# Dilated attention: scores of the two heads of a pair issued in turn on the two halves of the array rows, items two by two every second slot

## What is computed

```python
def dilated_mixer(h, w_in, w_out):
    proj = (h @ w_in).reshape(B, S, N_GROUPS, 3, N_HEADS, HEAD_DIM)   # 3 groups, q/k/v, 16 heads of 64
    for g, (window, dil) in enumerate(((128, 1), (512, 4), (2048, 16))):
        q, k = partial_rotary(proj[:, :, g, 0], pos), partial_rotary(proj[:, :, g, 1], pos)
        o, lse = dilated_band_attention(q, k, proj[:, :, g, 2], dil, window // dil)
    wts = softmax(stack(lses)); o = einsum('gbsh,gbshd->bshd', wts, stack(outs))
    return o.reshape(B, S, ATTN_WIDTH) @ w_out
```

## Time and profile before

| | |
|---|---|
| median of three runs | 2191.45 us |
| the profiled execution | 2191.2 us, with a span of 2189.4 us |
| mean granted TensorE clock | 0.981 of full speed |
| TensorE matmul busy | 2077.3 us (95%) |
| VectorE busy | 1226.0 us (56%) |
| ScalarE busy | 1011.4 us (46%) |
| DMA | 354.16 MB, 162 GB/s |

### The profile page before, as it was taken

How to read it: one execution, slowest core, us unless ns; L and a number is a source line. 1 busy time by engine, 2 the same in 40 slices (tenths; PEclk the granted TensorE clock), 3 DMA queues, 4 the chain that set the end, 5 groups by cost and what they waited for, 6 DMA issues and landing times.

```text
span 2189.4 us, 27184 instructions
## 1 busy us (share of the span) xinstructions
PE 2077.3 (95%) x9866; PEld 1711.1 (78%) x9866; DVE 1226.0 (56%) x1352; ACT 1011.4 (46%) x1257; POOL 237.8 (11%) x351
## 2 busy tenths in 40 slices
PE   6999988989999999979999999999999999999997
PEld 5887867778887887867778877888878887888886
DVE  4555579865455555579865554444445545445544
ACT  4444663544444435754544444444435444454442
POOL 1000067000000000086000001111100000000000
PEclk9999999999999999999999999999999999999999
DMA  5554442545544554442444544333334554414552
GB/s 226 203 184 172 173 151 97 186 157 192 187 182 176 179 191 182 158 155 97 183 172 182 187 177 154 120 131 119 130 118 154 191 189 148 163 58 178 187 192 86
DMA packets 53861, 354.16 MB, mean 162 GB/s; under 512 B 7824, under 2 KB 8464, under 8 KB 11920
## 3 DMA queue, kind: packets, MB, share of 16 engines
q1 hardware_dynamic: 53776, 353.04, 43.8%
HBM read 351.97 MB, written 1.05 MB: 161 GB/s over the span
## 4 chain that ended last, share of the span: by engine, by line
PE 81%; DVE 8%; ACT 4%; issue 3%; DVEq 2%; POOL 1%; POOLq 1%; DMA 0%; ACTq 0%; SPq 0%
PE psum L1641 56%; PE psum L1697 16%; DVE wlo L959 3%; DVE arena L1134 2%; DVEq L1128 2%; ACT whi L551 2%; PE psum L1707 1%; PE psum L2038 1%; PE psum L1739 1%; PE psum L2018 1%; PE psum L1653 1%; PE psum L2025 1%; POOL arena L1509 1%; PE psum L1787 1%; PE psum L1816 0%
## 5 line engine op out<-in xcount | busy, mean ns | idle before, releaser
L959 DVE TENSOR_TENSOR wlo<-raw,whi 128x2048 fp32r<-128x2048 f32 x325 | 744.3, 2292 | 441.4 <-ACT whi L551 441.1
L1641 PE MATMUL psum<-whi,xTh 128*128 128x512 f32 (+1 forms) x1936 | 776.3, 401 | 30.7 <-DVE xTl L966 17.5
L1641 PE MATMUL psum<-whi,xTl 128*128 128x512 f32 (+1 forms) x1936 | 755.3, 390 | 0.0
L1641 PE MATMUL psum<-wlo,xTh 128*128 128x512 f32 (+1 forms) x1936 | 754.1, 389 | 0.0
L551 ACT ACTIVATE whi<-raw 128x2048 fp32r<-128x2048 f32 x325 | 621.0, 1916 | 272.6 <-PE psum L1697 151.0
L1641 PEld LDWEIGHTS psum<-whi,xTh 128*128 128x128 f32 x1936 | 368.2, 190 | 108.4 <-DVE xTl L966 17.4
L1641 PEld LDWEIGHTS psum<-whi,xTl 128*128 128x128 f32 x1936 | 367.7, 190 | 77.6
L1641 PEld LDWEIGHTS psum<-wlo,xTh 128*128 128x128 f32 x1936 | 368.9, 191 | 68.6
L1697 PE MATMUL psum<-whi,braT 128*128 128x512 f32 x1056 | 337.4, 390 | 6.6 <-DVE braT L1078 6.6
L1697 PEld LDWEIGHTS psum<-whi,braT 128*128 128x128 f32 x1056 | 198.2, 188 | 49.0 <-issue 5.4
L1697 PE MATMUL psum<-wlo,braT 128*128 128x512 f32 x528 | 205.5, 389 | 0.0
(11 more groups left out here) (214 smaller groups left out, 1553.3 us busy)
## 6 DMA issues: line engine op xcount, KB each, us to landing
raw<-w_stream SPq DMA_DIRECT2D x327, 1024.0 KB, 4.8
bias<-chunks SPq DMA_DIRECT2D x18, 256.0 KB, 4.9
x<-x_in SPq DMA_DIRECT2D x1, 1024.0 KB, 5.1
arena<-gate_w SPq DMA_DIRECT2D x2, 512.0 KB, 4.8
arena<-fins SPq DMA_DIRECT2D x2, 512.0 KB, 5.5
out<-x SPq DMA_DIRECT2D x1, 1024.0 KB, 4.0
con<-consts SPq DMA_DIRECT2D x1, 720.0 KB, 11.6
vec<-vecs SPq DMA_DIRECT2D x2, 94.5 KB, 3.9
```

What stands on the lines that cost most here:

```text
L959: TT(wlo[:, r], raw[:, r], whi[:, r].bitcast(F32), ALU.subtract).then_inc(lo_done, 1)
L1641: ins = pe.matmul(dst(rb), s(kt)[:, rows], w[:, r, at_:at_ + cols], start=start and n == 0 and k == 0, stop=stop and n == len(kts) - 1 and ...
```

## The change

Two consecutive items become the two heads of a pair on the same block of queries (before: the two blocks of one head). `dil_item` maps an item number to (head, block). `DIL_TWO` starts two items in every second slot (6, 8, ... 16, 20, ... 34) where `DIL_ITEM` started one in each slot. `scores_of(first)` issues both: two masks, then for each group the matmul of head one (rows 0 to 63, bank 4) and of head two (rows 64 to 127, bank 5). It waits until both previous items are out. The other engines do their two steps one after the other; the last of the 28 items of the loop is now finished within the loop.

```diff
-DIL_ITEM = {dil_first_slot(p) + n: 4 * p + n for p in range(PAIRS - 1) for n in range(4)}
+DIL_TWO = {dil_first_slot(p) + 2 * n: 4 * p + 2 * n for p in range(PAIRS - 1) for n in range(2)}
+
+
+def dil_item(i):
+
+    pair_, n = divmod(i, 4)
+    return 2 * pair_ + n % 2, n // 2
+
+
...
 # ScalarE, in slot k
-                    if DIL_ITEM.get(k - 1, 1) % 2 == 0:
-                        turned_out(DIL_ITEM[k - 1])
-                    if k in DIL_ITEM:
-                        exp(DIL_ITEM[k])
+                    if k - 1 in DIL_TWO:
+                        turned_out(DIL_TWO[k - 1])
+                    if k in DIL_TWO:
+                        exp(DIL_TWO[k])
+                        exp(DIL_TWO[k] + 1)
...
 # VectorE, in slot k
-                    if k in DIL_ITEM:
-                        largest(DIL_ITEM[k])
-                    if DIL_ITEM.get(k - 1, 0) % 2:
-                        turned_out(DIL_ITEM[k - 1])
+                    if k in DIL_TWO:
+                        largest(DIL_TWO[k])
+                        largest(DIL_TWO[k] + 1)
+                    if k - 1 in DIL_TWO:
+                        turned_out(DIL_TWO[k - 1] + 1)
                     if k:
                         split(b, k)
                     if half and u:
                         tiles_out(u - 1, 1)
-                    if k - 1 in DIL_ITEM:
-                        o_out(DIL_ITEM[k - 1])
+                    if k - 1 in DIL_TWO:
+                        o_out(DIL_TWO[k - 1])
+                        o_out(DIL_TWO[k - 1] + 1)
...
                 v_out(NDIL - 1)
-                turned_out(last - 1)
                 split(b, k)
-                o_out(last - 1)
...
 # TensorE
-                    if i >= 2:
-                        pe.wait_ge(item_out, i - 1)
-                    bank_, rows = psum[:, 4 + i % 2], slice(HD * half, HD * half + HD)
-                    q = lambda g: d_T[pair_ % 3][rows, g, blk * P:(blk + 1) * P]
-                    k = lambda g: d_T[pair_ % 3][rows, GROUPS + g]
-                    pe.matmul(bank_, identb[:], maskb[:, 2 * P + blk * W:2 * P + (blk + 1) * W], start=True, stop=False)
-                    pe.matmul(bank_[:, 0:S], q(0), k(0), start=False, stop=False)
-                    pe.matmul(bank_[:, S:S + P], q(1), k(1)[:, blk * P:(blk + 1) * P], start=False, stop=False)
-                    pe.matmul(bank_[:, S + P:W], q(2), k(2)[:, blk * P:(blk + 1) * P], start=False, stop=True).then_inc(s_in, 1)
+                    if first >= 2:
+                        pe.wait_ge(item_out, first)
+                    banks = [psum[:, 4], psum[:, 5]]
+                    rows = [slice(0, HD), slice(HD, 2 * HD)]
+                    own = slice(blk * P, (blk + 1) * P)
+                    for bank_ in banks:
+                        pe.matmul(bank_, identb[:], maskb[:, 2 * P + blk * W:2 * P + (blk + 1) * W], start=True, stop=False)
+                    for g, cols, keys in ((0, slice(0, S), slice(0, S)), (1, slice(S, S + P), own), (2, slice(S + P, W), own)):
+                        for bank_, r in zip(banks, rows):
+                            ins = pe.matmul(bank_[:, cols], d_T[pair_ % 3][r, g, own], d_T[pair_ % 3][r, GROUPS + g][:, keys], start=False, stop=g == 2)
+                            if g == 2:
+                                ins.then_inc(s_in, 1)
...
-                            if n == 1 and i - 1 in DIL_ITEM:
-                                turn_p(DIL_ITEM[i - 1])
+                            if n == 1 and i - 1 in DIL_TWO:
+                                turn_p(DIL_TWO[i - 1])
+                                turn_p(DIL_TWO[i - 1] + 1)
...
-                            if n == 3 and i - 1 in DIL_ITEM:
-                                pv(DIL_ITEM[i - 1])
+                            if n == 3 and i - 1 in DIL_TWO:
+                                pv(DIL_TWO[i - 1])
+                                pv(DIL_TWO[i - 1] + 1)
...
 # behind the loop: turn_p(last - 1) and pv(last - 1) go; scores_of(last + 1), scores_of(last + 3) are now within scores_of(last), scores_of(last + 2)
```

More of the change, by code:

```diff
@@ L96 @@
 DIL_TURNS += [(f"t{NDIL - 1}.0", "act"), ("o4", "split"), ("o5", "split")]
-assert max(DIL_ITEM) == 2 * NDIL - 1 and len(dil_groups(NDIL - 1)) == 1
+assert max(DIL_TWO) == 2 * NDIL - 2 and all(k % 2 == 0 for k in DIL_TWO) and len(dil_groups(NDIL - 1)) == 1
 FOX_TURNS = (NORM_TURNS + [(f"{qk}{n}", "act" if n % 2 == 0 else "dve") for qk in "qk" for n in range(8)]
@@ L833, in exp @@
                 def exp(i):
-                    h, blk = divmod(i, 2)
                     act.wait_ge(max_done, b.head * 2 + i + 1)
@@ L1363, in o_out @@
                 def o_out(i):
-                    h, blk = divmod(i, 2)
+                    h, blk = dil_item(i)
                     dve.wait_ge(exp_done, b.head * 2 + i + 1)
@@ L1997, in dil, with scores_of @@
                 first_ready = x_ready(b)
[L1999 to L2003, removed]
+                def scores_of(first):
+                    pair_, blk = dil_item(first)[0] // 2, dil_item(first)[1]
+                    if first % 4 == 0:
                         u = dil_unit_of(pair_, "k", GROUPS - 1)
@@ L2032, in pv @@
                         pe.wait_ge(udve, b.udve + units.upto(f"u{dil_unit_of(pair_, 'v', GROUPS - 1)}", "both"))
-                    if blk:
-                        pe.wait_ge(pt_dve, h + 1)
+                    if i % 2:
+                        pe.wait_ge(pt_dve, i // 2 + 1)
                     else:
-                        pe.wait_ge(pt_act, b.head + h + 1)
+                        pe.wait_ge(pt_act, b.head + i // 2 + 1)
                     for n, (g, kb) in enumerate(((0, 0), (0, 1), (1, blk), (2, blk))):
@@ L2072, in dil @@
                                     tile_turns(u - 1, 0)
-                                if i in DIL_ITEM:
-                                    scores_of(DIL_ITEM[i])
-                            if n == 1 and i - 1 in DIL_ITEM:
-                                turn_p(DIL_ITEM[i - 1])
+                                if i in DIL_TWO:
+                                    scores_of(DIL_TWO[i])
+                            if n == 1 and i - 1 in DIL_TWO:
+                                turn_p(DIL_TWO[i - 1])
+                                turn_p(DIL_TWO[i - 1] + 1)
                             if n == 2:
@@ L2098, in dil @@
                 out(0, 1)
-                turn_p(last - 1)
                 out(0, 2)
@@ L2102, in dil @@
                 out(0, 3).then_inc(slot_used, 1)
-                pv(last - 1)
                 out(1, 0)
                 scores_of(last)
-                scores_of(last + 1)
                 out(1, 1)
@@ L2116, in dil @@
                 scores_of(last + 2)
-                scores_of(last + 3)
                 out(0, 5)
```

## The result

The changed kernel takes 2169.91 us (median of 5 runs, 2169.43 to 2170.46), the kernel before 2191.45 in the same job: a ratio of 0.9899, with a 95% interval of 0.9886 to 0.9912. It is 21.5 us faster. The forecast was a gain of 13.4 us and a range of 2173.5 to 2186.5 us.

A forecast was written before the change was run, and what follows sets the result against it. TensorE's own instruction list was taken to bound the kernel. Fewer row changes save 6.4 us and, with load-bound overlap of the halves, 13.4 us in all; other terms zero: 2178.0 us from 2191.45, range 2173.5 to 2186.5.

The forecast's parts named there:

- What bounds it: In the dilated mixer stage, time is what TensorE spends on its own list; TensorE busy all 60.00 us from 1550 to 1610.
- The serial sum: Scores of a pair without overlap take 2.57 us instead of 2.98 in the loop or 2.89 at the end, saving 6.4 us.
- row changes: Switching the array between 128 and 64 rows around the scores costs 0.20 us each way; two per pair of items go.
- The overlap of the halves: The 12 score passes, 1.72 us serially, fall to 1.28 us bounded by weight loads, 0.44 us less a pair; chance 0.38.
- best case: In-order bound on a pair's 12 score passes, each starting after the last pass has started: 1.07 us, 0.65 us less.
- full-overlap rival: Loads of both halves run beside each other within the in-order bound, saving 16.8 us, to 2174.7 us; chance 0.22.
- The loads: Score weight loads go one after another whatever the half, 0.106 us each; half the rows do not make one shorter.
- Merged blocks of `turn_p` and `pv`: Putting two items' transposes and `pv` side by side, 14 merged blocks of each, saves nothing on TensorE.
- slow stretch: Stretch behind the seam pause at mean granted clock 0.66; stays, begins by chance, 1.7 us either way if gone or doubled.
- Draining at a change of half: Rival: in the scores, five changes of half a pair cost 0.20 us each; 9.6 us slower, 2201.1 us; chance 0.10.
- The wait for both items: `scores_of(first)` waiting for both previous items costs 0; rival, VectorE late: 12 us given back, near 2190, chance 0.06.
- The seam: Around 1610 us TensorE pauses for VectorE's `v_out` of the last unit; pause again 1.7 us, sum 0.

The follow-up runs named there:

- both items on one half: Changed kernel, but a pair's two items are one head's two query blocks, so all 12 score passes use the same 64 rows; 2183.43 us, ratio to before 0.9958.
- head after head: Changed kernel, but after both masks all six passes of head one come before all six of head two; 2180.32 us, ratio to before 0.9944.
- the run with two groups: Changed kernel, reordered to groups 0 and 1 of head one, the same of head two, then group 2 of each; 2171.14 us, ratio to before 0.9904.
- the two profiles without the pause: Changed kernel with TensorE's wait for the last projection unit moved behind the output projection's first four k-steps; 2167.61 us in both runs, ratios 0.9887 and 0.9891.

## Why the prediction came out as it did

- **What bounds it**: right. TensorE's own list set the time of the stage before and after, and between 1357 and 1600 us the only wait of its matmul queue is the pause at the seam.
- **The serial sum**: right. 2.57 us forecast for a pair without overlap, 2.59 measured on one half; the row changes are worth what rows 4 said.
- **The overlap of the halves: wrong, and this is the step that failed.** I bounded the overlap by an in-order start ("a pass of B starts as soon as the last pass of A has started") and took a value inside that bound from `pv`'s load rate, 12 x 0.106 = 1.28 us. Both parts were wrong. The 12 passes take 0.88 us, half of the serial 1.72: head two does not wait for head one's second pass, and the loads of the two halves start 7 ns apart, so `pv`'s 0.106 us is the rate of one list, not of the engine. Predicted gain of the term 0.44 us a pair, measured 1.72 - 0.88 = 0.84 (0.88 against the kernel with both items on one half): 0.40 x 16 = 6.4 us of the 7.5 missing in the stage (20.9 against 13.4). The "best case" of 1.07 us was no bound either, and so the full-overlap rival of 2174.7 and the range's low end were too high as well. The full parallel price was there to be taken from the rows: half of 1.72 is 0.86 us, which gives (0.41 + 0.86) x 14 + (0.32 + 0.86) x 2 = 20.1 us, or 2171.3.
- **The rule cited for full overlap.** The Trainium skill, "TensorE: Matmul & The Clock Gate", section "Part 3: Packing small matmuls — row/col tiling", has matmuls on different row groups start about 4 ns apart. The trace agrees in kind: 7 ns here, 13 ns where four passes of head one stand ahead. I had given full overlap a chance of 0.22, and clipped its size by the in-order bound. The same section of the Trainium skill has matmuls start and end strictly in program order. Matmul by matmul the changed kernel keeps this order of starts; my error was to ask it of each pass. In the experiment with head after head the order of starts breaks for whole matmuls too: head two's first started at 1614.685, head one's third after it. The ends are modelled in the profile, and no run here settles them.
- **The loads.** The Trainium skill, "TensorE: Matmul & The Clock Gate", section "LDWEIGHTS (loading the stationary operand)", has a load's time go by its columns and not by its rows. The 188 ns listed for 64 rows and the 190 for 128 agree with it. It is about one load; that the loads of the two halves run side by side is what the 7 ns between them show.
- **Merged blocks of `turn_p` and `pv`**: taken as nothing, and right: together less than 0.1 us. The 0.9 us that the stage gained beyond the scores had no term in my sum; two thirds of it lie in the product matmuls, which stand farther from a block on average, and 0.2 us in the slow stretch.
- **Draining at a change of half**: ruled out by 2169.91 us and by the two starts 7 ns apart. The Trainium skill, "TensorEngine Tiling (Array Packing)", section "Tiling Modes", has a change of mode drain the engine and a change of the tile alone not. The trace agrees: going from 128 rows to 64 or back costs 0.2 us, and changing the half nothing that shows.
- **The wait for both items**: right, it never shows. A slot of the changed kernel, first TensorE, then VectorE:

```profile
1451.01 1.89 PE L2048 MATMUL psum<-arena 128*128 128x64 f32 x16
1452.71 0.48 PE L1649 MATMUL psum<-whi,xTh 128*128 128x512 f32 x1
```
```profile
1450.80 0.68 DVE L1355 TENSOR_SCALAR arena<-psum 128x512 f32<-128x512 f32 x1
...
1452.94 0.28 DVE L1378 TENSOR_SCALAR arena<-psum,small 128x64 f32<-128x64 f32 x1 [0.54 <-PE psum L2048]
```

VectorE is through with its other work in time and ends the second scaling at 1453.22 us, 0.51 us after TensorE left `pv`, where a k-step of 1.4 us lies ahead of a mask.

- **The seam**: the pause stayed at 1.67 us for a forecast of 1.7. That its slow stretch comes and goes by chance was said, and two profiles of one program show it.

## What to carry to other kernels

Two float32 matmuls with 64 rows on the two halves of the array, writing to two banks, cost the time of one, loads included, if they stand close to each other in the program with no 128-row matmul between: alternate them, or let no more than two matmuls of one half stand ahead of the other's, as in the run with two groups. Count row changes as work (0.2 us each way here), and gather them. When a bound rests on how instructions are ordered inside an engine and no row shows that case, keep the full parallel price as an end of the range.

## What the runs showed of the hardware that was not expected

- Head two's first pass started 7 ns after head one's first with one waiting pass of head one between them in the program, and 13 ns after it with three, but not past four or five: with all six ahead it began 0.54 us later, with head one's third.
- Weight loads of the two halves run beside each other: the first and the last of the 12 start 0.77 us apart (1604.12 and 1604.89 by their records), where `pv` on all rows, at 0.106 us a load, needs 11 x 0.106 = 1.17.
- After the same pause of 1.67 us the granted clock fell to a mean of 0.67 over 5.2 us in one profile (for part of it matmuls came 0.43 instead of 0.23 us apart, at 1.2 instead of 2.4 GHz) and stayed at 1.00 in another of the same program. In the two profiles without the pause it was 1.00 behind the seam.
